# Layer 1: the first eight heads between the projection units of the last eight

## The chip, the core and the metric

The program runs on one core of one Trainium2 chip. A core has a tensor engine (PE), a vector engine (DVE), a scalar engine (ACT), a gpsimd engine (POOL) and a sync engine (SP) that issues transfers. Each engine works off its own queue in order and waits for the others through semaphores. The metric is the device time of one execution in microseconds (us). The kernel before takes 1052.06 us in the median of three runs (1048.58 to 1052.34).

## What is computed

Two blocks of two layers each, on 256 tokens of width 1024, in float32. The change is in layer 1 of the first block: normalise, project to q, k and v of 16 heads of width 64, turn q and k by position (rope), attend with a causal mask that holds the logarithm of how many of three patterns contain a key, project out, add. Cut to that:

```python
h = rms_norm(x, attn_norm[1])
q, k, v = split(h @ w_qkv_o)                  # 3 x 16 heads x 64
q, k = apply_rope(q, cos, sin), apply_rope(k, cos, sin)
for window, dil in ((128, 1), (512, 4), (2048, 16)):
    o, lse = banded_attention(strided(q), strided(k), strided(v), window // dil)
o = sum(softmax(lses) * outs)                 # merged by the softmax denominators
x = x + o @ w_out_o
x = x + silu_gated_ffn(rms_norm(x, ffn_norm[1]))
```

## The kernel before

**Split weights.** Float32 products are made of three products of rounded halves. Weights stream in units of 128 x 1024 elements through a ring of 8 slots: SP issues the transfer into `w_raw`, ACT makes the high half (`w_hi`, line 600), and DVE (line 885) or, for units listed in `POOL_UNITS`, POOL (line 492) makes the low half `w_lo` over the raw data. A slot is free again when PE has used the unit. ACT and DVE work four units ahead (`AHEAD`). `w_qkv_o` has 6 chunks of 512 columns and 4 units each, `w_out_o` has 2 chunks of 4 units. One unit is 12 matmuls on PE: 2 token tiles x 2 slices x 3 products (lines 1468 to 1470).

**Projection.** PE's `chunk` adds four units up in a pair of PSUM banks; ACT (line 654) and DVE (line 944) copy the sums to `z`, a token tile each. Chunks alternate between bank pair 0, 1 and bank pair 2, 3. Chunks 0 and 1 are q, 2 and 3 are k, 4 and 5 are v. After chunks 0 to 3 DVE's `rotate` applies rope (lines 977 to 984) and signals `qk1_ready`; after each of chunks 1 to 4 PE transposes two fills (`transpose_blocks`, line 1447). A fill is one PSUM bank of transposed blocks, numbered on through the whole program; even ones are drained by ACT (line 646), odd ones by DVE (line 934), and PE opens a fill only when the last one of its parity is drained (`open_fill`).

**Attention.** Only when all six chunks are done does `attention("attn1")` run over 16 heads, on each engine as one loop over steps. For every head: scores on PE (S, line 1609); mask, negative maximum and copy to SBUF on DVE (line 1017); two exponentials with row sums on ACT (lines 700 and 702); reciprocal and two scalings on DVE (lines 1058, 1065, 1066; the helper `scale_probs`); three transposes on PE (T, line 1654) into a fill; a copy to `probT` by ACT (line 715, even fills) or DVE (line 1041, odd fills); product with v on PE (PV, line 1634). For each pair of heads ACT (line 740) and DVE (line 1084) write the high and low half of the result to `hT_hi` and `hT_lo`. Then `project_out` multiplies with `w_out_o`, and the residual, norm and feed-forward follow. The 8 units of `w_out_o` are POOL's (line 492).

Of the kernel before, what the change touches and what calls it, by code (L numbers as in the profile page):

```python
# [5 lines left out]
F32 = mybir.dt.float32  # L6
# [28 lines left out]
def cut(lo, hi):  # L35
# [7 lines left out]
    "w_qkv_o": (cut(0, 3072), []),  # L43
# [62 lines left out]
FILL, _f = {}, 0  # L106
for _name, _n in [("norm0", 4), ("prep0", 11), ("cmp_p", 1), ("attn0", 24), ("norm1", 4), ("norm2", 4),
                  ("prep1", 8), ("attn1", 16), ("norm3", 4), ("norm5", 4), ("prep2", 7), ("attn2", 16),
                  ("norm6", 4), ("lora", 2), ("prep3", 12), ("attn3", 16)]:
    FILL[_name] = _f  # L110
    _f += _n
# [26 lines left out]
def net(nc, a, out):  # L138
# [30 lines left out]
    gains = place("gains", [P, GAIN_COLS])  # L169
    gtab = place("gtab", [P, NT, 4, HD])  # L170
    gb = place("gb", [P, D])
# [4 lines left out]
    w2 = place("w2", [P, 2, 192])  # L176
# [7 lines left out]
    reg = place("reg", [P, 24, T])  # L184
    prob_at = cursor[0]
    prob = place("prob", [P, 3, 512])
    probT = place("probT", [P, 2, 512])
# [224 lines left out]

    def bank_taken(p):
# [18 lines left out]
    POOL_UNITS = {st: (next_units(st), next_units(st) + RING) for st in STAGES}  # L432
# [40 lines left out]
    def _(pool):  # L473
# [37 lines left out]
        pool.wait_ge(t_filled, FILL["norm0"] + 4)  # L511
# [10 lines left out]
        split("attn1")  # L522
# [66 lines left out]
    def _(act):  # L589
# [28 lines left out]
        def high(k, t):  # L618

            for q in range(2):  # L620
                f = FILL[f"norm{k}"] + 2 * t + q
# [18 lines left out]
        def drain(stage, fills):  # L640
            for k in fills:
                f = FILL[stage] + k
# [6 lines left out]
        def take(name, c, dst, dense=None, done=None):  # L649
# [4 lines left out]
            n.activation(dst[0][:, 0, lo:lo + w], ps[:, 2 * (d % 2), 0:w], ACT.Copy).then_inc(acc_free[0], 1)  # L654
# [6 lines left out]
        def gate_chunks(name, which, dense):  # L661

            for g, c in enumerate(which):
# [3 lines left out]
                for b in range(4):  # L667
                    d = dense + 2 * g + b // 2
                    n.activation(gT[:, 4 * g + b, :], ps[:, 2 * (d % 2) + b % 2, 0:T], ACT.Silu)\
# [19 lines left out]
        def attention(stage):  # L689
            inst, i0, f0 = INST[stage], INST0[stage], FILL[stage]  # L690
            base = next_units(stage)
            for s in range(len(inst) + LAG + 5):
                if s < len(inst):
# [5 lines left out]
                    src, sign = (ps, 1.0) if it["bias"] is None else (prob, -1.0)  # L699
                    n.activation(prob[:, i % 3, 0:w], src[:, i % 3, 0:w], ACT.Exp, bias=negm[:, i, 0:1],  # L700
                                 scale=sign, accum_out=den[:, i, 0:1])
                    n.activation(prob[:, i % 3, 256:512], src[:, i % 3, 256:512], ACT.Exp, bias=negm[:, i, 1:2],
# [6 lines left out]
                if 0 <= j < len(inst) and (f0 + j) % 2 == 0:  # L709
# [5 lines left out]
                    n.activation(probT[:, i % 2, 0:w], ps[:, TB, 0:w], ACT.Copy).then_inc(t_drained[0], 1)  # L715
# [1198 lines left out]
```

## Times and profile before

| | before |
|---|---|
| median of three runs | 1052.06 us |
| the profiled execution, its own time | 1052.18 us |
| its span in the trace | 1050.4 us |
| TensorE clock granted, mean | 0.946 |
| DVE busy | 63% of the span |
| ACT busy | 46% of the span |

How to read the profile: busy time says how long an engine worked in a stretch; what a stretch is worth has to be read from the waits in it. Start times are counted from the span's start. The time of a matmul in the list is a latency; what it costs in a stream is the spacing of starts. A granted clock of 1.00 is 2.4 GHz, 0.50 is 1.2 GHz. The 1.8 us between span and device time lie around the program.

### The profile page before, as it was taken

The numbers are of one execution on the slowest core, as the hardware profiler recorded it, in microseconds if no ns is written. First come the engines' busy times: TensorE is split into PE (matmuls) and PEld (weight loads), VectorE is DVE, ScalarE is ACT, GpSimd is POOL, SyncE is SP. The second block draws the span as 40 slices with busy tenths as digits, with TensorE's granted clock in tenths as the row PEclk, the third lists the DMA queues.
The fourth block names the chain that finished last, engine by engine and source line by source line (L and its number), as shares of the span: only waits on it lengthen the run. The fifth ranks groups of instructions, "written<-read, shape, count | busy, mean of one in ns | idle before, by whom it ended". The sixth has DMA issues, their size and how long they took to land. (4 is left out here: it accounts for less than half of the span.)

```text
span 1050.4 us, 14873 instructions
## 1 busy us (share of the span) xinstructions
PE 934.8 (89%) x5660; PEld 795.0 (76%) x5660; DVE 664.3 (63%) x1200; ACT 484.5 (46%) x887; POOL 180.1 (17%) x129
## 2 busy tenths in 40 slices
PE   5995778899999999987899999998998799786878
PEld 4784446799998878855699999886887478586657
DVE  4778894456555458757545555546874947848672
ACT  5343653445454344455445545434544635442640
POOL 2004020000000000051000000003655300518430
PEclk9997779899999999989999999998999999998789
DMA  8463002465566657520546555656752036452001
GB/s 316 133 213 139 1 1 81 131 200 171 177 203 209 189 164 217 181 84 13 174 131 203 164 181 205 208 169 172 246 170 94 1 93 203 141 144 97 1 1 40
DMA packets 96790, 148.69 MB, mean 142 GB/s; under 512 B 6272, under 2 KB 59680, under 8 KB 96592
## 3 DMA queue, kind: packets, MB, share of 16 engines
q1 hardware_dynamic: 94512, 140.50, 42.6%
q10 hardware_dynamic: 1296, 4.83, 1.4%
q0 software_dynamic: 912, 2.41, 0.9%
q8 instruction: 45, 0.74, 0.3%
q14 instruction: 25, 0.20, 0.1%
HBM read 146.67 MB, written 1.05 MB: 141 GB/s over the span
## 5 line engine op out<-in xcount | busy, mean ns | idle before, releaser
L885 DVE TENSOR_TENSOR w_lo<-w_raw,w_hi 128x1024 fp32r<-128x1024 f32 (+2 forms) x230 | 272.3, 1208 | 150.3 <-ACT w_hi L600 147.3
L600 ACT ACTIVATE w_hi<-w_raw 128x1024 fp32r<-128x1024 f32 (+2 forms) x269 | 273.5, 1042 | 165.7 <-DMA w_raw<-in_w_gate_up 74.5
L1468 PE MATMUL ps<-hT_hi,w_lo 128*128 128x256 f32 x832 | 239.6, 288 | 8.5 <-POOL w_lo L492 4.6
L1469 PE MATMUL ps<-hT_hi,w_hi 128*128 128x256 f32 x832 | 239.1, 287 | 0.0
L1470 PE MATMUL ps<-hT_lo,w_hi 128*128 128x256 f32 x832 | 239.1, 287 | 0.0
L1468 PE MATMUL ps<-w_hi,hT_lo 128*128 128x512 f32 (+3 forms) x448 | 174.4, 389 | 9.2 <-DVE w_lo L885 4.4
L1469 PE MATMUL ps<-w_hi,hT_hi 128*128 128x512 f32 (+3 forms) x448 | 171.4, 383 | 0.0
L1470 PE MATMUL ps<-w_lo,hT_hi 128*128 128x512 f32 (+3 forms) x448 | 171.3, 382 | 0.0
L1468 PEld LDWEIGHTS ps<-hT_hi,w_lo 128*128 128x128 f32 x832 | 163.5, 196 | 9.6 <-issue 6.8
L1470 PEld LDWEIGHTS ps<-hT_lo,w_hi 128*128 128x128 f32 x832 | 163.4, 196 | 0.0
L1469 PEld LDWEIGHTS ps<-hT_hi,w_hi 128*128 128x128 f32 x832 | 163.2, 196 | 0.0
L492 POOL TENSOR_TENSOR w_lo<-w_raw,w_hi 128x1024 fp32r<-128x1024 f32 (+1 forms) x39 | 97.9, 2526 | 193.5 <-ACT w_hi L600 193.3
L1468 PEld LDWEIGHTS ps<-w_hi,hT_lo 128*128 128x128 f32 x448 | 85.9, 192 | 28.5 <-DVE w_lo L885 6.3
L1470 PEld LDWEIGHTS ps<-w_lo,hT_hi 128*128 128x128 f32 x448 | 85.7, 191 | 15.7
L1469 PEld LDWEIGHTS ps<-w_hi,hT_hi 128*128 128x128 f32 x448 | 85.8, 191 | 14.6
L1654 PE MATMUL ps<-table,prob 128*128 128x128 f32 x248 | 50.1, 326 | 35.1 <-DVE prob L1066 34.6
L1654 PEld LDWEIGHTS ps<-table,prob 128*128 128x128 f32 x248 | 30.5, 159 | 62.0 <-DVE prob L1066 52.7
L1468 PE MATMUL ps<-w_hi,hid_lo 128*128 128x512 f32 x176 | 69.6, 395 | 0.0
L1470 PE MATMUL ps<-w_lo,hid_hi 128*128 128x512 f32 x176 | 69.5, 395 | 0.0
L1469 PE MATMUL ps<-w_hi,hid_hi 128*128 128x512 f32 x176 | 69.5, 395 | 0.0
L498 POOL TENSOR_TENSOR small<-small 128x1 f32<-128x1 f32 x10 | 5.6, 556 | 326.6 <-DVE small L892 326.6
L654 ACT ACTIVATE z<-ps 128x512 f32<-128x512 f32 (+3 forms) x20 | 11.2, 562 | 93.1 <-PE ps L1470 93.1
(207 smaller groups left out, 1148.8 us busy)
## 6 DMA issues: line engine op xcount, KB each, us to landing
w_raw<-in_w_gate_up SPq DMA_DIRECT2D x176, 256.0 KB, 4.4
w_raw<-in_w_down SPq DMA_DIRECT2D x44, 512.0 KB, 4.2
w_raw<-in_w_in_e SPq DMA_DIRECT2D x38, 512.0 KB, 4.9
w_raw<-in_w_qkv_o SPq DMA_DIRECT2D x24, 512.0 KB, 4.0
w_raw<-in_w_in_o SPq DMA_DIRECT2D x20, 512.0 KB, 3.6
w_raw<-in_w_out_e SPq DMA_DIRECT2D x16, 512.0 KB, 5.1
w_raw<-in_w_out_o SPq DMA_DIRECT2D x16, 512.0 KB, 3.7
w_raw<-in_w_in_e SPq DMA_DIRECT2D x8, 268.0 KB, 2.7
```

Of the source, the lines that this page charges most:

```text
L492: g.tensor_tensor(w_lo[:, u % RING, 0:size], w_raw[:, u % RING, 0:size], w_hi[:, u % RING, 0:size].bitcast(F32), ALU.subtract).then_inc(po ...
L498: g.tensor_tensor(rstd[:, t:t + 1], ms[:, t:t + 1], halfs[:, 0:1], ALU.pow)\
L600: n.activation(w_hi[:, u % RING, 0:size], w_raw[:, u % RING, 0:size], ACT.Copy).then_inc(hi_ready, 1)
L654: n.activation(dst[0][:, 0, lo:lo + w], ps[:, 2 * (d % 2), 0:w], ACT.Copy).then_inc(acc_free[0], 1)
L885: v.tensor_tensor(w_lo[:, u % RING, 0:size], w_raw[:, u % RING, 0:size], w_hi[:, u % RING, 0:size].bitcast(F32), ALU.subtract).then_inc(lo ...
L1468: m.matmul(o, lhs[1], rhs[0], start=start, stop=False)
L1469: m.matmul(o, lhs[0], rhs[0], start=False, stop=False)
L1470: return m.matmul(o, lhs[0], rhs[1], start=False, stop=stop)
L1654: ins = m.transpose(ps[:, TB + f % 2, col:col + P], prob[:, i % 3, 256 * t + kt * P:256 * t + kt * P + P], ident)
```

## The change

The columns of `w_qkv_o` are taken in the order q, k, v of heads 0 to 7, then q, k, v of heads 8 to 15. After chunk 2, all four engines walk one table, `HEADS_1`, and each picks the events that are its own. `unit` is one projection unit (on ACT and DVE: the halves of the unit four further on), S n the scores, maxima and exponentials of heads 2n and 2n+1, SC n their scaling, T j the transposes and copy of head j, PV n and MIX n the product with v and the halves of the result, `take` the copy of a chunk's sums, `rope` the rotation, `fill` the transposes of q and k, `out` a unit of `w_out_o`.

```diff
-    "w_qkv_o": (cut(0, 3072), []),
+    "w_qkv_o": ([(1024 * p + 512 * half, 512) for half in range(2) for p in range(3)], []),
+SHARED = [DENSE["w_qkv_o"] + c for c in (3, 4, 5)]
+BANK = {d: 2 * (d % 2) for d in range(_d)}
+BANK.update({d: 0 for d in SHARED})
+for _name in OUTS:
+    BANK[DENSE[_name]], BANK[DENSE[_name] + 1] = 0, 2
+HEADS_1 = [("unit", 3, 0), ("unit", 3, 1), ("S", 0), ("unit", 3, 2), ("unit", 3, 3), ("SC", 0), ("take", 3), ("S", 1),
+           ("T", 0), ("T", 1),
+           ("unit", 4, 0), ("unit", 4, 1), ("SC", 1), ("rope", 3), ("S", 2), ("T", 2), ("T", 3), ("PV", 0),
+           ("unit", 4, 2), ("unit", 4, 3), ("SC", 2), ("take", 4), ("MIX", 0), ("S", 3), ("T", 4), ("T", 5), ("PV", 1),
+           ("unit", 5, 0), ("unit", 5, 1), ("SC", 3), ("rope", 4), ("fill", 2), ("fill", 3), ("MIX", 1), ("T", 6),
+           ("T", 7), ("PV", 2),
+           ("unit", 5, 2), ("MIX", 2), ("fill", 6), ("fill", 7), ("S", 4), ("unit", 5, 3), ("PV", 3), ("take", 5),
+           ("SC", 4), ("MIX", 3), ("S", 5), ("T", 8), ("T", 9),
+           ("out", 0), ("SC", 5), ("S", 6), ("T", 10), ("T", 11), ("PV", 4),
+           ("out", 1), ("SC", 6), ("MIX", 4), ("S", 7), ("T", 12), ("T", 13), ("PV", 5),
+           ("SC", 7), ("MIX", 5), ("T", 14), ("T", 15), ("PV", 6), ("MIX", 6), ("PV", 7), ("MIX", 7)]
-    POOL_UNITS = {st: (next_units(st), next_units(st) + RING) for st in STAGES}
+    POOL_UNITS = {st: (next_units(st), next_units(st) + RING) for st in STAGES if st != "attn1"}
-    prob = place("prob", [P, 3, 512])
-    probT = place("probT", [P, 2, 512])
+    prob = place("prob", [P, 4, 512])
+    probT = place("probT", [P, 4, 512])
```

The accumulators of chunks 3, 4 and 5 and of the first chunk of `w_out_o` share banks 0 and 1, since the scores now stand in banks 2 and 3, a head each: S n waits for the maxima of S n-1. `prob` and `probT` have four buffers. In layer 1 ACT alone makes the copies to `probT`, of both parities, and the result goes to buffers of its own (`mixed_hi`, `mixed_lo`), so that `hT` stays readable. The low halves of `w_out_o` move from POOL to DVE. On PE and DVE the walk is, in its main branches:

```diff
+                if what == "unit":
+                    split(FIRST["w_qkv_o", at[0]] + at[1] + 1 + AHEAD)
+                elif what == "out":
+                    split(FIRST["w_out_o", 0] + at[0] + 1 + AHEAD)
...
+                elif what == "rope":
+                    rope_1(at[0])
+                elif what == "fill":
+                    drain("prep1", at)
+                elif what == "S":
+                    maximum("attn1", 2 * at[0])
+                    maximum("attn1", 2 * at[0] + 1)
+                elif what == "SC":
+                    scale_probs("attn1", 2 * at[0])
+                    scale_probs("attn1", 2 * at[0] + 1)
...
+        def transposed(stage, j):
+
+            i, f, causal = INST0[stage] + j, FILL[stage, j], INST[stage][j]["causal"]
+            pe.wait_ge(probs_ready, i + 1)
+            open_fill(f)
```

**Where instructions stand.** First DVE, before, from the end of chunk 2 to the halves that follow: the sums, rope, the odd fill, four low halves.

```order
L944 COPY z<-ps 128x512 [waits units_used]
L977 TENSOR_TENSOR tmp<-z,table 128x16x32 [waits acc_free_1,acc_free_0]
L979 TENSOR_TENSOR tmp<-z,table 128x16x32
L982 TENSOR_TENSOR z<-z,table 128x2x512 [waits dve_chain]
L984 TENSOR_TENSOR z<-z,tmp 128x2x512 [waits dve_chain]
L934 COPY reg<-ps 128x512 [waits dve_chain,t_filled]
L885 TENSOR_TENSOR w_lo<-w_raw,w_hi 128x1024 [waits hi_ready] x4
```

DVE in the change, at the table's `unit 5,0` to `MIX 2`: two low halves, SC 3 (six rows, the last three shown), rope 4, the odd fill (fill 3), MIX 1.

```order
L967 TENSOR_TENSOR w_lo<-w_raw,w_hi 128x1024 [waits hi_ready] x2
...
L1184 RECIPROCAL fac<-den 128x2 [waits exp_ready]
L1191 TENSOR_SCALAR prob<-prob,fac 128x128 [waits dve_chain]
L1192 TENSOR_SCALAR prob<-prob,fac 128x256
L1059 TENSOR_TENSOR tmp<-z,table 128x16x32 [waits acc_free_1,acc_free_0]
L1061 TENSOR_TENSOR tmp<-z,table 128x16x32
L1064 TENSOR_TENSOR z<-z,table 128x2x512 [waits dve_chain]
L1066 TENSOR_TENSOR z<-z,tmp 128x2x512 [waits dve_chain]
L1016 COPY reg<-ps 128x512 [waits dve_chain,t_filled]
L1211 TENSOR_TENSOR mixed_lo<-ps,mixed_hi 128x256 [waits mix_hi]
```

The odd fill still follows a rope, and in front of both now stand the scalings of two heads.

PE in the change, at the table's `fill 2` to `unit 5,2`: fills 2 and 3 (line 1573), T 6 and T 7 (line 1784), PV 2 (line 1769), the next unit.

```order
L1573 MATMUL ps<-table,z 128x128 [waits t_drained_even,qk1_ready]
L1573 MATMUL ps<-table,z 128x128 x3
L1573 MATMUL ps<-table,z 128x128 [waits t_drained_odd,qk1_ready]
L1573 MATMUL ps<-table,z 128x128 x3
L1784 MATMUL ps<-table,prob 128x128 [waits t_drained_even,probs_ready]
L1784 MATMUL ps<-table,prob 128x128 x2
L1784 MATMUL ps<-table,prob 128x128 [waits t_drained_odd,probs_ready]
L1784 MATMUL ps<-table,prob 128x128 x2
L1769 MATMUL ps<-probT,z 64x256 [waits t_drained_odd,t_drained_even,mix_lo]
L1769 MATMUL ps<-probT,z 64x256
L1769 MATMUL ps<-probT,z 64x128 x2
L1594 MATMUL ps<-w_hi,hT_lo 128x512 [waits lo_ready]
```

Before, only projection units stood behind a pair of fills; now a head's transposes do, in the same two banks.

ACT in the change, from S 3 to the units' high halves behind it (`S 3`, `T 4`, `T 5`, `unit 5,0`, `unit 5,1`, the even fill).

```order
L825 ACTIVATE prob,den<-prob,negm 128x128 [waits max_ready]
L827 ACTIVATE prob,den<-prob,negm 128x256
L825 ACTIVATE prob,den<-prob,negm 128x128 [waits max_ready]
L827 ACTIVATE prob,den<-prob,negm 128x256
L837 ACTIVATE probT<-ps 128x384 [waits pv_done,t_filled] x2
L643 ACTIVATE w_hi<-w_raw 128x1024 [waits units_used,slot_full_6]
L643 ACTIVATE w_hi<-w_raw 128x1024 [waits units_used,slot_full_7]
L689 ACTIVATE reg<-ps 128x512 [waits t_filled]
```

Two heads' exponentials and two copies stand in front of the weights' high halves; before, the four high halves of a chunk stood in a row with nothing of the attention near them.

## Rows read from the trace of the kernel before

**Rows 1.** Busy time by stage; columns in the first line, then one stage a line.

```profile
core 0: us, PE busy (x) PEld busy (x) DVE busy (x) ACT busy (x) POOL busy (x), PEclk, DMA share, GB/s
420.80:455.50 34.70, 34.70 (x163) 28.59 (x160) 20.12 (x22) 14.02 (x17) 9.48 (x4) 1.00 0.59 180
455.50:493.30 37.80, 27.57 (x177) 16.43 (x176) 32.05 (x128) 26.33 (x85) 9.41 (x4) 0.82 0.05 16
493.30:504.20 10.90, 10.90 (x50) 9.03 (x49) 1.65 (x2) 2.36 (x3) 0.00 (x0) 1.00 0.41 126
```

**Rows 2.** Timeline of PE, two fills, then projection units: start, time, line, shapes.

```profile
420.00 1.03 PE L1447 MATMUL ps<-table,z 128*128 128x128 f32 x8
420.80 0.48 PE L1468 MATMUL ps<-w_hi,hT_lo 128*128 128x512 f32 x1
```

**Rows 3.** Timeline of PE in the attention's last part and the first out unit.

```profile
485.76 0.93 PE L1609 MATMUL ps<-reg 64*128 64x128 f32 x8
486.65 0.55 PE L1654 MATMUL ps<-table,prob 128*128 128x128 f32 x3
487.21 0.87 PE L1634 MATMUL ps<-probT,z 128*64 128x256 f32 x8
...
492.52 0.87 PE L1634 MATMUL ps<-probT,z 128*64 128x256 f32 x8 [0.74 <-DVE probT L1041]
493.32 0.50 PE L1468 MATMUL ps<-w_hi,hT_lo 128*128 128x512 f32 x1
```

**Rows 4.** Timeline of DVE: rope of one chunk, a fill, four low halves.

```profile
409.23 0.69 DVE L977 TENSOR_TENSOR tmp<-z,table 128x512 f32<-128x512 f32 x1
...
413.19 0.69 DVE L934 COPY reg<-ps 128x512 f32<-128x512 f32 x1
413.80 4.62 DVE L885 TENSOR_TENSOR w_lo<-w_raw,w_hi 128x1024 fp32r<-128x1024 f32 x4
```

**Rows 5.** Timeline of DVE: one head of attention, the next head's start, a low half.

```profile
459.77 0.28 DVE L1017 CUSTOM_DVE_ANT_0 prob<-ps,table 128x128 f32<-128x128 f32 x1
...
460.32 0.16 DVE L1058 RECIPROCAL fac<-den 128x2 f32<-128x2 f32 x1
...
460.99 0.28 DVE L1017 CUSTOM_DVE_ANT_0 prob<-ps,table 128x128 f32<-128x128 f32 x1
...
484.97 0.42 DVE L1084 TENSOR_TENSOR hT_lo<-ps,hT_hi 128x256 fp32r<-128x256 f32 x1
```

**Rows 6.** Timeline of ACT: four high halves, two heads' first exponentials, a copy.

```profile
432.96 3.91 ACT L600 ACTIVATE w_hi<-w_raw 128x1024 fp32r<-128x1024 f32 x4
...
458.09 0.40 ACT L700 ACTIVATE prob<-prob,negm 128x128 f32<-128x128 f32 x1 [0.64 <-DVE negm L1017]
...
458.98 0.39 ACT L700 ACTIVATE prob<-prob,negm 128x128 f32<-128x128 f32 x1
...
461.33 0.47 ACT L715 ACTIVATE probT<-ps 128x384 f32<-128x384 f32 x1
461.70 0.39 ACT L700 ACTIVATE prob<-prob,negm 128x128 f32<-128x128 f32 x1
```

**Rows 7.** Timeline of POOL and DVE where both work.

```profile
463.70 2.36 POOL L492 TENSOR_TENSOR w_lo<-w_raw,w_hi 128x1024 fp32r<-128x1024 f32 x1 [8.35 <-ACT w_hi L600]
...
464.40 1.74 DVE L1065 TENSOR_SCALAR prob<-prob,fac 128x128 f32<-128x128 f32 x1
```

**Rows 8.** Busy time and granted clock of single microseconds, columns as in Rows 1.

```profile
460.00:461.00 1.00, 0.46 (x3) 0.22 (x3) 0.96 (x8) 0.56 (x3) 0.00 (x0) 0.80 0.00 0
470.00:471.00 1.00, 1.00 (x8) 0.47 (x4) 1.00 (x1) 0.64 (x4) 1.00 (x1) 0.58 0.00 0
...
523.00:524.00 1.00, 1.00 (x5) 1.00 (x6) 0.48 (x1) 0.91 (x1) 0.00 (x0) 0.50 0.75 213
528.00:529.00 1.00, 1.00 (x7) 1.00 (x7) 0.81 (x1) 0.28 (x1) 0.00 (x0) 0.56 0.01 4
```

**Rows 9.** Waits of PE in the attention: for whom, total us, times, longest.

```profile
PE ps L1654 <- DVE prob L1066: 7.6, 9, 1.9
```

More of the change, by code:

```diff
@@ L786, in _ @@
         load_gain(3, 2)
-        for c in range(6):
-            chunk("w_qkv_o", c, z1)
-            if 1 <= c < 5:
-                drain("prep1", range(2 * c - 2, 2 * c))
-        attention("attn1")
+        chunk("w_qkv_o", 0, z1)
+        chunk("w_qkv_o", 1, z1)
+        drain("prep1", (0, 1))
+        chunk("w_qkv_o", 2, z1)
+        drain("prep1", (4, 5))
+        heads_1()
         projection_out("w_out_o")
@@ L929, in drain @@
             for k in fills:
[L930 removed]
+                f = FILL[stage, k]
                 if f % 2:
@@ L1049, in attention, with maximum, heads_1, rope_1 @@
                     at_step(s)
+        def maximum(stage, j):
+            i, it = INST0[stage] + j, INST[stage][j]
+            dve.wait_ge(scores_ready, i + 1)
+            if j >= 4:
+                dve.wait_ge(t_filled, FILL[stage, j - 4] + 1)
+            for t in range(NT):
+                w = P * (t + 1) if it["causal"] else T
+                cols = slice(256 * t, 256 * t + w)
+                ins = v.tensor_tensor_reduce(out=prob[:, i % 4, cols], in0=ps[:, 2 + i % 2, cols], in1=it["bias"](t),
+                                             scale=-1.0, scalar=-4.0 * NEG, op0=ALU.add, op1=ALU.min,
+                                             accum_out=negm[:, i, t:t + 1])
+            ins.then_inc(max_ready, 1)
+        def heads_1():
+            for what, *at in HEADS_1:
+                if what == "unit":
+                    split(FIRST["w_qkv_o", at[0]] + at[1] + 1 + AHEAD)
+                elif what == "out":
+                    split(FIRST["w_out_o", 0] + at[0] + 1 + AHEAD)
+                elif what == "take":
+                    take(DENSE["w_qkv_o"] + at[0], z1, *COLS["w_qkv_o"][0][at[0]], LAST["w_qkv_o", at[0]])
+                elif what == "rope":
+                    rope_1(at[0])
+                elif what == "fill":
+                    drain("prep1", at)
+                elif what == "S":
+                    maximum("attn1", 2 * at[0])
[3 more added lines that the diff above has]
+                    scale_probs("attn1", 2 * at[0] + 1)
+                elif what == "MIX":
+                    mix_low("attn1", 2 * at[0] + 1)
+        def rope_1(c):
+            wait_taken("w_qkv_o", c + 1)
+            lo = COLS["w_qkv_o"][0][c][0]
+            sec = heads(z1[:, :, lo:lo + 512])
+            rotate(sec, [sec], rope_q if lo < 1024 else rope, 8, 32)
+            dve.sem_inc(sem("qk1_ready"), 1)
         def scale_probs(stage, j):
@@ L1215, in _ @@
         norm_second(2, EPS_1)
-        for c in range(6):
-            chunk("w_qkv_o", c, z1)
-            if c < 4:
-                sec = heads(z1[:, :, 512 * c:512 * c + 512])
-                rotate(sec, [sec], rope_q if c < 2 else rope, 8, 32)
-                dve.sem_inc(sem("qk1_ready"), 1)
-            if 1 <= c < 5:
-                drain("prep1", range(2 * c - 2, 2 * c))
-        attention("attn1")
+        chunk("w_qkv_o", 0, z1)
+        rope_1(0)
+        chunk("w_qkv_o", 1, z1)
+        rope_1(1)
+        drain("prep1", (0, 1))
+        chunk("w_qkv_o", 2, z1)
+        drain("prep1", (4, 5))
+        heads_1()
         projection_out("w_out_o", 2, 3, EPS_1)
```

265 lines of the change are left out of this document (167 added, 98 removed).

## Prediction, written before the change was run

> **What bounds the kernel now.** I read the stages first [rows 1]. In the projection PE is busy all the time: 34.7 of 34.7 us in chunks 3 to 5, at full clock. In the attention it is busy 27.6 of 37.8 us, at a mean clock of 0.82, and the first chunk of `w_out_o` is dense again from 493.3 to 504.2. So the idle time is in the attention, and what ends most of it is the scaling of the probabilities on DVE: 7.6 us in 9 waits [rows 9]. DVE is busy 32.1 of 37.8 us there, but only 20.1 of 34.7 us beside chunks 3 to 5, and ACT 14.0 [rows 1]: there is room in the projection for attention work. Part of DVE's time is a block by POOL: a low half on POOL from 463.70 to 466.06 holds DVE's scaling, begun at 464.40, for 1.74 us [rows 7]; the same scaling takes 0.2 us from start to start elsewhere. There are four such halves in the stage.
>
> **Prices.** On PE, start to start at full clock: a unit 2.72 us (10.9 us for four [rows 1]), two fills 0.80 [rows 2], scores of two heads 0.89, transposes of a head 0.56, a pair's PV 0.80 [rows 3]. On DVE: maxima of a head 0.55, its scaling 0.67, a result's low half 0.35, a weight's low half 1.16, rope 3.96, a copy of 512 columns 0.61 [rows 4, 5]. On ACT: exponentials of a head 0.89, a copy to `probT` 0.37, a high half 0.98 [rows 6].
>
> **What would be won if PE never waited.** From the start of chunk 3, at 420.8 in both [rows 2] (the order of the first three chunks leaves two pairs of fills before it in both, and the rope that goes from behind chunk 2 only frees DVE), PE has up to the end of the first chunk of `w_out_o` 16 units 43.5, two pairs of fills 1.6, scores 7.1, transposes 8.5, PV 6.4: 67.1 us, end at 487.9 instead of 504.2. That is the whole prize, 16.3 us. After that point nothing changes: the next transfers into the ring, the residual add and the norm follow the units of that chunk as before, so an end moved by d moves the program by d.
>
> **What it costs: the order on DVE and ACT.** The table puts work of the weights and of the heads into one in-order queue on each of the two, and each waits for the other within one period. From the maxima of S n to those of S n+1: maxima of the first head 0.55, two heads' exponentials 1.78, two copies to `probT` 0.75 (these sit on ACT behind the exponentials), the first high half with its handover 1.1, two low halves 2.32, SC 1.34. That is 7.84 us in which nothing of PE appears. I add this chain up in the clock of the trace of before:
>
> - S 0's maxima: 420.8 + two units 5.44 + scores 0.85 = 427.1.
> - To S 1: 7.84, without the copies (-0.75), with the take of chunk 3 (+0.61): 434.8.
> - To S 2: 7.84 and rope 3, which stands ahead of S 2: 3.96. 446.6.
> - To S 3: 7.84, take 0.61, MIX 0.35: 455.4. PE ended unit 4,3 at about 449.7 and the scores of S 3 at 450.6, and T 4 waits for SC 2's first head at about 453.7: 3 us idle.
> - To fill 3 drained: 7.84, rope 4 3.96, the copy 0.69: 467.9. Here is the longest wait. T 7 writes the bank that fill 3 was in, and DVE drains fill 3 only behind rope 4. PE is through with unit 5,1 and both fills at about 462 and with T 6 at 463, so it is idle nearly 5 us.
> - To S 4's maxima: now PE is the path: T 7 0.56, PV 2 0.80, unit 5,2 2.72, fills 6 and 7 0.80, their drain 0.65, scores 0.85: 474.3.
> - To S 5: 0.55, 1.78, high half 1.1, one low half 1.16, take 0.61, SC 1.34, MIX 0.35: 6.9, at 481.2. To S 6: no take and no MIX, but two copies: 6.7, at 487.9. To S 7: 7.0, at 494.9. PE has a unit, scores, two T and a PV in such a period, 5.5 us: it waits, with 1 to 2.5 us of slack.
> - To the end: 0.55, 1.78, 0.67 to the scaling of head 15, 497.9; T 15 0.56 and two PV 1.60, 500.0; two units of `w_out_o` 5.45: 505.5.
>
> Against 504.2 that is 1.3 us later: the waits, some 17.6 us in sum, eat the whole prize. The table-load and the exponentials hidden beside chunk 3 are in the chain; the low halves of `w_out_o` that DVE takes from POOL are 1.16 each in it, and the blocks by POOL are gone from it. The step I trust least is the sum of handovers, taken from start-to-start times; 2 us either way.
>
> **The clock.** In the trace the clock falls to 0.50 at 460 to 461, in the attention's thin beginning, and is back at 1.00 only late in 470 to 471; and before the feed-forward, where PE had waited for the norm, a dense stream runs at 0.50 from 523 until 528.9 [rows 8]. Such a stretch at half clock costs a PE-bound stream half its length. The change removes the first stretch (it is inside the 37.8 us, so its price is already in the comparison), and makes a new gap of 5 us before T 7. I expect the fall there. T 7 to the fills are 4.9 us of work at full clock and all on the path. The bounds are nothing and 4.9 us; I take the dense case's length of 5.6 us, hence 2.8 us, since what follows T 7 is a stream like that one. The fall that I also expect behind the gap before T 4 is hidden: units 5,0 and 5,1 and the fills have until 467.9.
>
> Sum: 1.3 + 2.8 = 4.1 us. The profiled execution took 1052.2 (span 1050.4 and 1.8 around it), the median is 1052.06, the same to 0.1; forecast 1056.3.
>
> **The rest at no cost.** Banks 0 and 1 shared by chunks 3, 4, 5: PE's next unit waits for the take, but S n+1 and two T stand between, and the chain already holds the take. Scores in two banks: S n waits for maxima that are over by then. The other three attentions get more buffers with unchanged waits. The transfers: the ring's slots come free as before, and in the attention DMA was at 0.05 [rows 1].
>
> **Rivals.**
>
> - The clock also falls at the tail. Between PV 5 (495.9) and 500 PE has only T 14, T 15 and the first of PV 6 and 7, and the two units behind them are on the path. Another 2.8 us: 1059.1. For it: a thin stretch like 459 to 461. Against it: in before the end of the attention was as thin and 493.3 to 504.2 is at 1.00 [rows 1]. The Trainium skill, "TensorE: Matmul & The Clock Gate", Part 4 on PE-mode transposes, says that transposes do not count as activity for the clock as matmuls do. By that rule this tail, where half the work is transposes, falls and the time is the 1059.1 of this rival; no row here separates transposes from other work, so it only adds to the chance.
> - The clock stays up, or the gap before T 7 is shorter: 1.3 us alone, 1053.5, and with the chain 2 us too long 1051.
> - The change does what its words say and PE hardly waits: 1035.9. This needs DVE and ACT to run ahead of the chain. Against it: rope 4 stands in the queue before the drain, in any timing.
> - Slower by one mechanism: PE stays at half clock from T 7 on for as long as the longest stretch seen, 10 us [rows 8]. Then T 7 to the fills cost 4.9 more, and with S 4 and unit 5,3 at half clock (7.2 us) `take 5` is no longer hidden by the 5.4 us of the exponentials and halves beside it: 1.8 more. With 1.3 that is 8.0: 1060.2. It decides from the point where unit 5,3 at half clock ends later than DVE's low half.
>
> **How the numbers follow.** Forecast 1056.3 with 0.42 (its own spread 1053.8 to 1058.8), the tail's clock 0.20, the clock up 0.17, as meant 0.06, the long half clock 0.15. A change of over 0.5%, 5.3 us, is about what a measurement can tell from none; its bound above is 1057.3. Above it lie 0.12 of the forecast, 0.17 of the second and 0.14 of the last: slower 0.43. Faster (under 1046.8) is the case as meant and a little of the clock case, 0.10. The rest, 0.47, is within. The range from 1049.5 to 1062 leaves out the case as meant and the outer parts of two others.
>
> **What would show it.** Right: PE idle about 5 us before the transposes of head 7, ended by DVE's copy to `reg`; about 3 us before T 4, ended by DVE's scaling; PE waiting 1 to 2 us in each of the last four periods of about 7 us; PE busy well under all of 421 to 500; low clock behind T 7; DVE's scaling nowhere over 0.4 us. Wrong: a wait before T 7 under 2 us, or a first chunk of `w_out_o` that ends before 500. If it ends near 505 but the time differs, the error is behind that point, where I expect no change.

## The result, and the profile after

| | before | after |
|---|---|---|
| median | 1051.69 us (20 runs) | 1058.72 us (20 runs) |
| lowest, highest | 1047.77, 1058.06 us | 1047.37, 1066.66 us |
| the profiled execution | 1052.18 us, span 1050.4 | 1057.84 us, span 1056.0 |
| mean granted clock in it | 0.946 | 0.945 |

The ratio after to before is 1.0055, with a 95% interval of 1.0034 to 1.0076: 3.6 to 8.0 us slower, 5.8 in the middle. The medians of the table are 7.0 us apart; they hold all 20 executions of after, while the ratio leaves out the two slowest (1066.08 and 1066.66 us). The forecast was 1056.3 us, 4.1 slower than before; the measured median lies 2.4 us above it, within the forecast's range of 1049.5 to 1062.

To compare layer 1 alone, this text uses its **length**: from the second pair of fills, at 420.00 in before [rows 2] and 425.57 in after, to the first transposes of the norm behind `w_out_o`, at 515.04 and 524.78. It is 95.0 us before and 99.2 after, 4.2 longer. Times of after are moved back by 5.57 us where they are set against those of before.

First the stages, at the clock times of [rows 1] (columns as there). They cut the same intervals from the span, though the program is 5.6 us behind:

```profile
core 0: us, PE busy (x) PEld busy (x) DVE busy (x) ACT busy (x) POOL busy (x), PEclk, DMA share, GB/s
420.80:455.50 34.70, 33.44 (x170) 25.63 (x168) 21.93 (x52) 15.36 (x38) 0.00 (x0) 1.00 0.47 148
455.50:493.30 37.80, 28.43 (x151) 20.14 (x150) 21.88 (x60) 18.02 (x47) 0.00 (x0) 0.91 0.22 74
493.30:504.20 10.90, 7.60 (x50) 4.90 (x48) 7.28 (x30) 4.51 (x15) 0.00 (x0) 1.00 0.32 96
```

PE's idle time was in the middle stage alone, 10.2 us; now it is in all three, 13.9 us. DVE, busy 32.05 of 37.80 us before, is busy 21.88: it is not the bound by its busy time any more, nor is ACT. POOL has left the stage. Now the waits of PE in layer 1 of after (for whom, total us, times, longest), which answer to [rows 9]:

```profile
PE ps L1784 <- DVE prob L1192: 8.9, 5, 3.4
PE ps L1784 <- DVE reg L1016: 3.1, 1, 3.1
PE ps L1784 <- ACT probT L837: 1.9, 1, 1.9
PE ps L1743 <- ACT reg L689: 0.8, 1, 0.8
```

The nine waits of at most 1.9 us for the scaling (7.6 us in all) have become five, of up to 3.4 (8.9 in all), and one of 3.1 for the odd fill's bank has come. The timeline of PE shows where they are (start, latency, line, shapes, idle before and who ended it): the transposes of T 4, T 6 and T 7, and then one wait in each of the last four periods. A **period** here is the time from the maxima of S n on DVE to those of S n+1. The first of the five waits, 0.93 us at T 2, is not shown.

```profile
459.94 1.21 PE L1784 MATMUL ps<-table,prob 128*128 128x128 f32 x6 [3.40 <-DVE prob L1192]
...
470.40 0.52 PE L1784 MATMUL ps<-table,prob 128*128 128x128 f32 x3 [0.34 <-ACT reg L689]
474.04 0.52 PE L1784 MATMUL ps<-table,prob 128*128 128x128 f32 x3 [3.12 <-DVE reg L1016]
...
488.59 1.20 PE L1784 MATMUL ps<-table,prob 128*128 128x128 f32 x6 [1.46 <-DVE prob L1192]
...
495.64 1.21 PE L1784 MATMUL ps<-table,prob 128*128 128x128 f32 x6 [2.20 <-DVE prob L1192]
...
502.37 1.21 PE L1784 MATMUL ps<-table,prob 128*128 128x128 f32 x6 [0.87 <-DVE prob L1192]
506.27 0.89 PE L1784 MATMUL ps<-table,prob 128*128 128x128 f32 x6 [1.89 <-ACT probT L837]
```

Why DVE's scaling is late can be read on ACT's and DVE's own timelines of after. One turn: the maxima of S 2 on DVE, exponentials, copies and high halves on ACT, low halves and the scaling SC 2 on DVE.

```profile
452.60 0.29 DVE L1142 CUSTOM_DVE_ANT_0 prob<-ps,table 128x128 f32<-128x128 f32 x1 [0.25 <-DVE z L1066]
...
453.28 0.40 ACT L825 ACTIVATE prob<-prob,negm 128x128 f32<-128x128 f32 x1 [7.41 <-DVE negm L1142]
...
455.05 0.84 ACT L837 ACTIVATE probT<-ps 128x384 f32<-128x384 f32 x2
455.79 1.99 ACT L643 ACTIVATE w_hi<-w_raw 128x1024 fp32r<-128x1024 f32 x2
...
456.87 2.36 DVE L967 TENSOR_TENSOR w_lo<-w_raw,w_hi 128x1024 fp32r<-128x1024 f32 x2 [3.07 <-ACT w_hi L643]
459.15 0.16 DVE L1184 RECIPROCAL fac<-den 128x2 f32<-128x2 f32 x1
...
461.39 0.28 DVE L1142 CUSTOM_DVE_ANT_0 prob<-ps,table 128x128 f32<-128x128 f32 x1
```

DVE is idle for 3.07 us before the low halves, because the first high half stands on ACT behind exponentials and copies that begin only with DVE's maxima; ACT was idle for 7.41 us before the exponentials. Each of the two waits for the other in every period, and the scaling, whose inputs were there from 455.2 on, stands behind the low halves till 459.15. The sum over the sixteen heads of after (426.3 to 515 us), two rows of the waits of all engines:

```profile
ACT prob L825 <- DVE negm L1142: 28.6, 8, 7.4
DVE w_lo L967 <- ACT w_hi L643: 22.8, 10, 3.1
```

### The profile page after: what moved, and what is told of

Read it like the earlier page. It is cut to its first block and busy times, and to the rows that moved or that the text cites. A ratio compares the mean times of both kernels' runs of the same rounds, so it can differ in the third digit from the quotient of the medians.

```text
span 1056.0 us, 14877 instructions
## 1 busy us (share of the span) xinstructions
PE 935.9 (89%) x5660; PEld 794.0 (75%) x5660; DVE 662.5 (63%) x1200; ACT 487.1 (46%) x895; POOL 160.5 (15%) x121
## 5 line engine op out<-in xcount | busy, mean ns | idle before, releaser
L967 DVE TENSOR_TENSOR w_lo<-w_raw,w_hi 128x1024 fp32r<-128x1024 f32 (+2 forms) x238 | 282.1, 1209 | 167.8 <-ACT w_hi L643 164.4
L1594 PE MATMUL ps<-w_hi,hT_lo 128*128 128x512 f32 (+3 forms) x416 | 163.1, 392 | 8.5 <-DVE w_lo L967 4.4
L1595 PE MATMUL ps<-w_hi,hT_hi 128*128 128x512 f32 (+3 forms) x416 | 159.3, 383 | 0.0
L1596 PE MATMUL ps<-w_lo,hT_hi 128*128 128x512 f32 (+3 forms) x416 | 159.0, 382 | 0.0
L1594 PEld LDWEIGHTS ps<-w_hi,hT_lo 128*128 128x128 f32 x416 | 80.2, 193 | 28.5 <-issue 6.8
L536 POOL TENSOR_TENSOR w_lo<-w_raw,w_hi 128x1024 fp32r<-128x1024 f32 (+1 forms) x31 | 78.7, 2554 | 120.9 <-ACT w_hi L643 120.6
L1596 PEld LDWEIGHTS ps<-w_lo,hT_hi 128*128 128x128 f32 x416 | 79.9, 192 | 14.8
L1595 PEld LDWEIGHTS ps<-w_hi,hT_hi 128*128 128x128 f32 x416 | 80.3, 193 | 13.4
L1784 PE MATMUL ps<-table,prob 128*128 128x128 f32 x248 | 47.0, 311 | 42.9 <-DVE prob L1192 36.6
L1743 PE MATMUL ps<-reg 64*128 64x256 f32 (+2 forms) x288 | 44.6, 408 | 5.4 <-ACT reg L689 2.6
```

The costliest lines, as they stand in the source:

```text
L536: g.tensor_tensor(w_lo[:, u % RING, 0:size], w_raw[:, u % RING, 0:size], w_hi[:, u % RING, 0:size].bitcast(F32), ALU.subtract).then_inc(po ...
L967: v.tensor_tensor(w_lo[:, u % RING, 0:size], w_raw[:, u % RING, 0:size], w_hi[:, u % RING, 0:size].bitcast(F32), ALU.subtract).then_inc(lo ...
L1594: m.matmul(o, lhs[1], rhs[0], start=start, stop=False)
L1595: m.matmul(o, lhs[0], rhs[0], start=False, stop=False)
L1596: return m.matmul(o, lhs[0], rhs[1], start=False, stop=stop)
L1743: ins = m.matmul(o, it["q"][:, t * P:(t + 1) * P], it["k"][:, 0:w], start=True, stop=True)
```

## The experiments

All are the changed kernel with one or two edits, except "only outside layer 1", in which layer 1 is as before. The lengths of layer 1 are from one profile each. Each ratio is to executions of the kernel before taken beside that kernel; for the experiments these were three sets, with medians of 1051.49 to 1053.30 us.

| kernel | layer 1, us | median, us | ratio | 95% interval |
|---|---|---|---|---|
| before | 95.0 | 1051.69 | | |
| after | 99.2 | 1058.72 | 1.0055 | 1.0034 to 1.0076 |
| fill before rope | 94.4 | 1051.88 | 1.0012 | 0.9981 to 1.0043 |
| only outside layer 1 | 95.7 | 1051.56 | 0.9996 | 0.9965 to 1.0027 |
| ACT two units ahead | 82.3 | 1037.92 | 0.9878 | 0.9834 to 0.9922 |
| the same, again | 82.4 | 1038.23 | 0.9880 | 0.9829 to 0.9930 |
| ACT one unit ahead | 88.8 | 1046.04 | 0.9940 | 0.9911 to 0.9969 |
| two ahead, fill before rope | 81.8 | 1040.84 | 0.9898 | 0.9855 to 0.9940 |
| one ahead, fill before rope | 84.0 | 1043.86 | 0.9916 | 0.9881 to 0.9952 |
| low halves on POOL | 93.2 | 1049.36 | 0.9976 | 0.9946 to 1.0006 |
| low halves on POOL, two ahead | 90.0 | 1045.48 | 0.9935 | 0.9899 to 0.9971 |
| high halves twice | 112.9 | 1065.66 | 1.0125 | 1.0091 to 1.0158 |
| high halves twice, two ahead | 86.7 | 1044.62 | 0.9939 | 0.9906 to 0.9972 |

### Is anything lost outside layer 1?

The profile of after is 6.05 us longer inside attention 0 (the attention of the first layer, from its first fills to the norm behind it), where the waits are nearly the same. So the parts outside layer 1 were kept, and layer 1 was put back:

```diff
-    "w_qkv_o": ([(1024 * p + 512 * half, 512) for half in range(2) for p in range(3)], []),
+    "w_qkv_o": (cut(0, 3072), []),
...
-SHARED = [DENSE["w_qkv_o"] + c for c in (3, 4, 5)]
...
-BANK.update({d: 0 for d in SHARED})
...
-    POOL_UNITS = {st: (next_units(st), next_units(st) + RING) for st in STAGES if st != "attn1"}
+    POOL_UNITS = {st: (next_units(st), next_units(st) + RING) for st in STAGES}
...
+        split("attn1")
...
```

> The changed kernel with layer 1 put back as before (column order, banks, hand-over of heads, GpSimd's share of the low halves), and with all that it changed elsewhere kept: four buffers of prob and probT, the banks of the out units, the second weight tile. Theory (all of the loss is in layer 1; the 6 us that the profile shows inside attention 0 are a clock that differs from execution to execution): ratio to the kernel before 0.999 to 1.001. Rival (the parts outside layer 1 cost something): 2 to 6 us over the kernel before, with the first attention longer in the profile.

Measured: 0.9996, layer 1 95.7 us. The parts outside cost nothing that can be measured (the interval reaches 3.5 us less to 2.8 us more); what is lost is lost in layer 1. The 6 us inside attention 0 are taken up in the last section.

### Does T 7 wait for DVE's order?

```diff
-           ("unit", 5, 0), ("unit", 5, 1), ("SC", 3), ("rope", 4), ("fill", 2), ("fill", 3), ("MIX", 1), ("T", 6),
+           ("unit", 5, 0), ("unit", 5, 1), ("SC", 3), ("fill", 2), ("fill", 3), ("rope", 4), ("MIX", 1), ("T", 6),
```

> One change in the table: VectorE drains the transposes of fills 2 and 3 before rope 4 instead of behind it, so that the bank that T7 needs comes free 3.96 us sooner. Theory (VectorE's order makes T7 late, and TensorE's clock falls behind that wait): T7 waits under 1 us, the granted clock stays at 1.00 behind it, and the eight exps of heads 8 to 15 come about 5.8 us earlier; less what the later waits for VectorE's scaling take back, the time is about 3 to 5 us below the changed kernel's (1058.7), so 1053.5 to 1055.5. Rival (T7's wait is slack, the chain of scalings is late on its own): no change against 1058.7. Rival (the rope is now what the scores of group 4 wait for): the wait moves from T7 to S4, time within 1 us of 1058.7.

Measured: layer 1 94.4 us, 4.9 shorter than after; ratio 1.0012, so some 4.5 us less than after, though the two intervals overlap (1.0034 to 1.0043). The wait of T 7 is gone, the clock stays at 1.00 where it fell behind T 7 in after, and what is left of after's waits is that of the chain, nearly unchanged:

```profile
PE ps L1784 <- DVE prob L1192: 8.8, 5, 3.4
PE ps L1784 <- ACT probT L837: 1.9, 1, 1.9
PE ps L1743 <- ACT reg L689: 1.1, 1, 1.1
```

The scores of S 4 start 51.2 us behind the second fills instead of 56.0. The theory holds by the profile: T 7's wait lay on the path. Neither rival does: the wait was no slack, and S 4's scores wait only 0.3 us longer for ACT's copy than in after.

### Is the period a chain between the two engines?

This is the main question, since by it the prediction let the whole prize go. ACT's high halves are moved in its own queue and nowhere else; DVE and PE walk the table as in after. The edit moves those of the whole table, not only those of heads 8 to 15 of which the expectation speaks.

```diff
                 if what == "unit":
-                    split(FIRST["w_qkv_o", at[0]] + at[1] + 1 + AHEAD)
+                    split(FIRST["w_qkv_o", at[0]] + at[1] + 3 + AHEAD)
                 elif what == "out":
-                    split(FIRST["w_out_o", 0] + at[0] + 1 + AHEAD)
+                    split(FIRST["w_out_o", 0] + at[0] + 3 + AHEAD)
```

> ScalarE makes the high halves of heads 8 to 15 two units further ahead in its own order, so that VectorE's low halves no longer stand behind a high half of the same period. Theory (the last periods of about 7 us are a chain that passes from VectorE to ScalarE and back: 7.84 us with the high half in it, 4.8 us without): the four periods behind S3 shrink from about 6.9 us to what TensorE needs, about 6 us or less; the end of layer 1 comes 3 to 6 us earlier, time 1052.5 to 1055.5. Rival (VectorE's busy time alone is the bound, whatever ScalarE's order): no change, 1058.7. Rival (the splits ahead now delay exp and the copies of transposed probabilities on ScalarE by 1.1 us each): later by 1 to 3 us.

Measured: 1037.92 us, ratio 0.9878, and on another chip 0.9880 with 1038.23 us.

> The kernel with ScalarE two units further ahead once more, on this chip, beside the two others: ratio 0.985 to 0.990 to the kernel before, the layer 82 to 83 us from the second fills to the norm. If its first ratio of 0.9878 was a matter of the chip or of few executions, it will lie above 0.992.

Layer 1 takes 82.3 us (82.4 again), 16.9 less than after and 12.7 less than before. The direction was right, the size three to five times too small in my expectation (3 to 6 us): I had looked only at the periods behind S 3, and all seven from S 0 to S 7 shrink. The same turn as above, maxima of S 2 to the scaling, now on DVE:

```profile
441.92 0.29 DVE L1142 CUSTOM_DVE_ANT_0 prob<-ps,table 128x128 f32<-128x128 f32 x1 [0.25 <-DVE z L1066]
...
443.04 2.35 DVE L967 TENSOR_TENSOR w_lo<-w_raw,w_hi 128x1024 fp32r<-128x1024 f32 x2
```

The low halves follow the maxima at once (443.04; in after 3.07 us of idle time lay between), because their high halves were made a period earlier, and the exponentials run beside them on ACT. DVE's waits for high halves fall from 22.8 us to this:

```profile
DVE w_lo L967 <- ACT w_hi L643: 4.0, 3, 2.3
```

And PE waits 3.5 us in the sixteen heads instead of 15.0 (the rows of after above, and those of 0.93 us at T 2 and 0.83 at S 4). One row without a wait, T 12 and T 13 at 479.87, is shown as well:

```profile
456.91 0.52 PE L1784 MATMUL ps<-table,prob 128*128 128x128 f32 x3 [0.34 <-ACT reg L689]
458.32 0.52 PE L1784 MATMUL ps<-table,prob 128*128 128x128 f32 x3 [0.89 <-DVE reg L1016]
...
464.29 0.93 PE L1743 MATMUL ps<-reg 64*128 64x128 f32 x8 [0.83 <-ACT reg L689]
...
479.87 0.88 PE L1784 MATMUL ps<-table,prob 128*128 128x128 f32 x6
...
483.03 0.89 PE L1784 MATMUL ps<-table,prob 128*128 128x128 f32 x6 [1.48 <-ACT probT L837]
```

The granted clock is 1.00 throughout:

```profile
420.00:455.00 35.00, 35.00 (x187) 26.86 (x186) 28.77 (x78) 24.36 (x56) 0.00 (x0) 1.00 0.45 141
455.00:501.00 46.00, 42.45 (x245) 31.71 (x244) 31.03 (x83) 25.11 (x66) 0.55 (x1) 1.00 0.30 98
```

Of the 16.9 us, 11.5 are waits of PE that are gone. Another 3.4 are stretches at half clock that are gone: in after, read in pieces of 2 us, the mean clock is 0.86, 0.50 and 0.79 behind T 4 and 0.77, 0.50 and 0.87 behind T 7, so each stretch lacks 1.7 us of work at full clock. Of the last 2.0 us some 1.8 are in the transposes. In after the scaling of T 13 ends at 502.97, behind the start of T 12 at 502.37, and the pair takes 1.13 us to the next work; with ACT ahead it takes 0.81 (479.87 to 480.68). The pairs at T 0, T 2, T 4, T 8 and T 10 lose 0.15 to 0.34 us in the same way. The prediction's case "PE hardly waits" had layer 1 at 95.0 - 16.3 = 78.7 us; with the 3.5 us of waits above it is 82.2, and 82.3 was measured. So the sum of PE's work was right, and all of the prize but these waits can be had with the table as it is. Its terms were not all right: transposes were priced at 0.56 us a head (and entered as 8.5 us, where 16 times 0.56 is 9.0), and a pair takes 0.81 here; a unit behind other work takes 2.86 (459.57 to 462.43) instead of 2.72.

### One unit, or two?

```diff
-                    split(FIRST["w_qkv_o", at[0]] + at[1] + 1 + AHEAD)
+                    split(FIRST["w_qkv_o", at[0]] + at[1] + 2 + AHEAD)
```

(the same for `out`).

> ScalarE only one unit further ahead. The chain theory by its own terms: of a period's two high halves one still stands behind the exps, so from maxima to maxima it takes 0.55 + 1.78 + 1.1 + 1.16 + 1.34 = about 5.9 us, under the 7 to 8 us that TensorE works in the periods with two units and about its 5.4 in the last ones: 0 to 2 us above the run with two units ahead, 1038 to 1040. Rival (the gain grows with each unit ahead, because what counts is the sum of high halves ahead of an exp): half of the 20.8 us, about 1048.

Measured: layer 1 88.8 us, ratio 0.9940; against the run with two ahead 6.5 us more in the profile and about the same by the ratios. I had expected 0 to 2, and the time, 1046.04 us, lies nearer to the rival's 1048 than to my 1038 to 1040. The waits tell why:

```profile
PE ps L1784 <- DVE reg L1016: 3.6, 1, 3.6
PE ps L1784 <- DVE prob L1192: 1.8, 1, 1.8
PE ps L1784 <- ACT probT L837: 1.5, 1, 1.5
```

In the last four periods there is no wait for the scaling, as the chain of 5.9 us had it. But the four periods before are longer than PE's work by a little each, with rope 3 and 4 in them, and this adds up to 1.8 us at T 4 and to a late rope 4, behind which the bank of T 7 is drained: 3.6 us and a stretch at half clock behind it. The term that I had left out of the expectation is rope 4. The next kernel puts that to the test, one unit ahead and the fills drained first:

> ScalarE one unit further ahead, and fills 2 and 3 drained ahead of rope 4. With one ahead alone layer 1 from the second fills to the norm took 88.8 us against 82.3 with two ahead; its trace shows 3.6 us for T7 and 1.8 us ahead of T4, and no other wait that the run with two ahead has not. Theory (the rest of the difference is T7's bank and the clock behind that wait, the period itself is under TensorE's): T7's wait goes, the layer takes 84 to 85 us, time 2 to 3 us above the run with two ahead, ratio 0.990. Rival (the period is still bound by the one high half that stands behind the exps): waits move to T8 to T15, layer 87 to 89 us, ratio 0.994 as before.

Measured: 84.0 us and 0.9916. T 7 does not wait, and of the waits listed above only the 1.8 and the 1.5 us stay; the rival's waits at T 8 to T 15 don't appear. It is the profile that decides here: the interval of the ratio, 0.9881 to 0.9952, holds both the 0.990 of the theory and the 0.994 of the rival. Both together, two units ahead and the fills first:

> ScalarE two units further ahead, and VectorE drains fills 2 and 3 ahead of rope 4. In the run with ScalarE ahead alone T7 still waited 0.9 us for the bank and nothing else in the heads waited for VectorE, so the theory gives 0.5 to 1 us less than its 1037.9: 1037 to 1037.5, not to be told from it. Rival (with the chain gone, rope 4 later makes the scores of group 4 late, since the register copies and the rope now stand closer to them): up to 3 us more, 1041.

Measured: layer 1 81.8 us, 0.5 shorter than with two ahead alone, as expected; the median, 1040.84 us, is 3 us above the 1037 to 1037.5 expected, and the ratio 0.9898 (0.9855 to 0.9940) can't be told from 0.9878. With the chain gone, rope 4's place is worth half a microsecond; with the chain, 4.9. The three kernels with the fills first also answer the rival of the kernel with one unit ahead, that each unit gains alike: from 94.4 us the first unit ahead takes 10.4, the second only 2.2.

### Does a high half cost where it stands?

While the heads are worked off, ACT makes each high half twice, 14 of them in the table as changed, and 16 with ACT two units ahead:

```diff
...
+                if in_heads_1[0]:
+                    n.activation(w_hi[:, u % RING, 0:size], w_raw[:, u % RING, 0:size], ACT.Copy)\
+                     .then_inc(sem("twice"), 1)
+                    doubled[0] += 1
+                    act.wait_ge(sem("twice"), doubled[0])
                 n.activation(w_hi[:, u % RING, 0:size], w_raw[:, u % RING, 0:size], ACT.Copy).then_inc(hi_ready, 1)
...
```

> The changed kernel with each high half of ScalarE made twice while the heads are worked off (the second write repeats the first), some 1.1 us more for each of 14. Chain theory: both high halves of a period lie on the chain VectorE, ScalarE, VectorE, so nearly all of them show: 10 to 15 us more than the changed kernel's 1058.7, 1069 to 1073. Rival (ScalarE is only half busy, 46.6 of 92 us, and its time is covered): 0 to 3 us more.

> The same doubling in the kernel with ScalarE two units further ahead. Chain theory: the high halves lie beside VectorE's low halves and the scaling now, and ScalarE's own work in a period (exps 1.78, copies 0.75, two doubled high halves 4.2, about 0.6 of other copies: 7.3 us) stays under TensorE's 7 to 8: 0 to 4 us above 1037.9, 1038 to 1042. Rival (each high half costs wherever it stands): 10 to 15 us more, 1048 to 1053.

Measured on the changed kernel: layer 1 112.9 us in the profile, 13.7 more than after, within the 10 to 15 expected; but the median, 1065.66 us, is below the 1069 to 1073 expected. The two largest of PE's waits there:

```profile
PE ps L1792 <- DVE prob L1200: 15.3, 7, 5.4
PE ps L1792 <- DVE reg L1024: 4.8, 1, 4.8
```

They have grown by 8.1 us, and with them the stretches at half clock. By the ratios, 1.0125 against 1.0055, the doubling costs only 7.4 us, with some 3 to 11.5 left open by the two intervals taken together; the profiled execution, 1077.05 us, is the longest of the six. So that it costs is shown; that it costs more than the rival's 0 to 3 us is shown by the profile and only just by the ratios. The size in a typical execution is open.

With ACT two units ahead the same doubling costs 4.4 us in the profile (86.7 against 82.3), just above the 0 to 4 expected (median 1044.62 us, expected 1038 to 1042). It has two places: a copy of the sums, which now stands behind two doubled high halves, and the last copy to `probT`.

```profile
PE ps L1792 <- ACT probT L843: 3.0, 1, 3.0
PE ps L1602 <- ACT z L703: 2.6, 1, 2.6
```

None of it is a wait for the scaling. In the profiles the pair says what the chain theory does (13.7 against 4.4 us for the same work or more). The ratios, 7.4 and 6.4 us with intervals of four to six us around each, don't tell the two apart, and by them alone this pair would be inconclusive.

### Would POOL have been the better place for the low halves?

```diff
-    POOL_UNITS = {st: (next_units(st), next_units(st) + RING) for st in STAGES if st != "attn1"}
+    POOL_UNITS = {st: (next_units(st), next_units(st) + RING) for st in STAGES}
...
+        split("attn1")
...
```

> The low halves of the out projection's splits in layer 1 go back to GpSimd, where the kernel before had them; nothing else. Theory (VectorE's in-order chain carries 1.16 us for each of these, two in a period): the last periods lose up to 2.3 us each if VectorE alone is late, so the time is 2 to 5 us below the changed kernel's. Rival (the GpSimd instruction of 1.74 us holds VectorE's scaling back while it runs, or its half is late for TensorE): the wait goes from VectorE's scaling to GpSimd's half, time the same within 1 us or up to 3 us above 1058.7.

> ScalarE two units further ahead, and the low halves of the out projection back on GpSimd. Theory (with the high halves ahead TensorE waits for neither engine, so it does not matter who makes the low halves): layer within 1 us of 82.3, ratio 0.987 to 0.989. Rival (GpSimd's 1.74 us instructions hold VectorE's maxima and scaling back, or GpSimd's 2.0 us a half come late for units that now follow each other sooner): TensorE waits for a low half or for scaling, layer 84 to 87 us, ratio 0.990 to 0.993.

Measured: in the changed kernel the move back helps, layer 1 93.2 us and 0.9976, 6.1 us less than after in the profile and some 8 by the ratios (expected 2 to 5). With ACT ahead the same move hurts: 90.0 us against 82.3; the ratios, 0.9935 against 0.9878 and 0.9880, point the same way with overlapping intervals. The second is the rival's case, by more than the rival said, and it is to be seen on two lines of DVE, one of POOL and one of PE in that kernel:

```profile
452.36 3.30 DVE L1065 TENSOR_TENSOR z<-z,table 128x1024 f32<-128x1024 f32 x1
455.69 3.25 DVE L1067 TENSOR_TENSOR z<-z,tmp 128x1024 f32<-128x1024 f32 x1
...
452.12 5.73 POOL L536 TENSOR_TENSOR w_lo<-w_raw,w_hi 128x1024 fp32r<-128x1024 f32 x2 [2.94 <-ACT w_hi L644]
...
459.92 0.88 PE L1785 MATMUL ps<-table,prob 128*128 128x128 f32 x3 [4.15 <-DVE reg L1017]
```

The two large steps of rope 4 take 3.30 and 3.25 us beside two low halves on POOL; with POOL idle they take 1.22 us each, in the run with ACT ahead at the same place:

```profile
454.85 1.22 DVE L1064 TENSOR_TENSOR z<-z,table 128x1024 f32<-128x1024 f32 x1
456.11 1.22 DVE L1066 TENSOR_TENSOR z<-z,tmp 128x1024 f32<-128x1024 f32 x1
```

POOL's two halves take 5.73 us together, where one takes 2.36 [rows 7]. The times fit each waiting for the other's instruction in turn: POOL's first half would end at 454.48, DVE's step of 1.22 us behind it at 455.70, POOL's second half at 458.06 and DVE's second step at 459.28; DVE's ended at 455.66 and 458.94, POOL's second half at 457.85. (The 1.74 us that the expectations give to GpSimd's instruction is DVE's held scaling in [rows 7], and no run has the 2.0 us a half; POOL's own take 2.35 to 2.39 where nothing holds them.) The Trainium skill, "SBUF — State Buffer", section "Who interferes with whom", says that VectorE and GpSimd share a pair of ports under an exclusive lock, and that a VectorE instruction with two SBUF inputs contends with a GpSimd instruction that reads SBUF; these rows agree, with 2.0 and 2.1 us more for two instructions of 1.22. The 4 us land just where T 7's bank is drained, and T 7 waits 4.15 us, 3.3 more than with POOL idle. Most of the rest of the 7.7 us is a wait of 1.71 us for the scaling at T 8, which that run does not have, and the half clock behind T 7: from T 7 to the scores of S 4 it is 8.20 us instead of 5.97.

In the changed kernel with ACT where it was, rope 4 is stretched in the same way (3.30 and 3.28 us), but low halves are taken out of DVE's chain, in the periods that wait for it: PE's waits for the scaling fall from 8.9 us in five to 6.0 in three, and T 7's from 3.1 to 1.7. So by the profiles the change was right to take the low halves from POOL, once the chain is undone, and wrong on that before.

## Why the prediction was right, step by step

Times of after are moved back by 5.57 us.

- **The in-order chain, 7.84 us a period plus rope and takes.** Forecast and measured starts or ends: maxima of S 0 427.1 and 427.4, S 1 434.8 and 435.1, S 2 446.6 and 447.0, S 3 455.4 and 455.8, fill 3 drained 467.9 and 468.3. Each step to within 0.4 us, and 0.3 of it is there from S 0 on. The idle time before T 4 was put at 3 us, ended by DVE's scaling: 3.40, so ended.
- **The longest wait, T 7.** Its cause was right (DVE's copy to `reg`, behind rope 4), and what it costs stood the test of its own experiment. Its length was not: 3.12 us instead of 5. PE came to T 6 later than 463, at 464.8, since it had done units 5,0 and 5,1 at half clock behind T 4. The text had this fall and called it hidden, which it was: T 7's time is set by DVE. It should then have shortened its own wait.
- **S 4, and the clock.** 474.3 with 2.8 for the clock, 477.1; measured 477.0. Here two terms were off in opposite directions, and that they met so closely is luck. From fill 3 drained to the maxima of S 4 the forecast had 6.4 us at full clock and 2.8 for half clock. With ACT two ahead, at full clock all the way, T 7 to the scores of S 4 takes 5.97 us, in after 7.57: the half clock cost 1.6 us, not 2.8. In two other kernels the same way took 7.52 (one unit ahead) and 8.20 us (two ahead, low halves on POOL), so it cost 1.6 and 2.2: the term was too large in each. The step that I took from the dense stretch of before [rows 8], 5.6 us long, was a guess by likeness; the stretch here is shorter (clock 0.50 in the first, 0.73 in the second of these two pieces of after):

```profile
475.00:477.00 2.00, 2.00 (x11) 1.30 (x8) 0.94 (x1) 1.36 (x3) 0.00 (x0) 0.50 0.01 4
477.00:479.00 2.00, 2.00 (x8) 1.60 (x7) 0.62 (x2) 0.00 (x0) 0.00 (x0) 0.73 0.00 0
```

  The work at full clock was counted too small, by some 0.6 us: the scores of S 4 wait 0.83 us for ACT's copy to `reg`, and the copy was in the sum at 0.65 without its handover.
- **The last four periods.** S 5 481.2 + 2.8 = 484.0 and 483.9, S 6 490.7 and 490.6, S 7 497.7 and 497.65. First of the last two units 502.8 and 503.1. The waits of 1 to 2.5 us were 1.46, 2.20, 0.87 and 1.89.
- **Nothing behind this point, nothing outside.** Layer 1 is 4.17 us longer in the profiles against 4.1 forecast, closer than terms that were off by about 1 us earn, and the kernel with only the parts outside layer 1 is at 0.9996.
- **The clock in before.** The prediction has one stretch at half clock in the attention of before, at 460 to 471. There is a second, behind waits of PE of 1.27 and 1.90 us, that it did not count:

```profile
480.00:482.00 2.00, 0.77 (x3) 0.50 (x3) 2.00 (x8) 0.26 (x1) 0.83 (x1) 0.77 0.01 4
482.00:484.00 2.00, 2.00 (x11) 1.29 (x11) 1.40 (x9) 1.25 (x5) 0.00 (x0) 0.50 0.00 0
```

  Like the first it lies within the length of before that the forecast compares with, so the sum is not touched.
- **The rivals.** The tail's clock didn't fall: it is 1.00 from 479.57 (unmoved) to the end of layer 1 in after. The page that the prediction quotes for this rival, the Trainium skill's "TensorE: Matmul & The Clock Gate", Part 4, made it likelier; after shows no fall in that tail, in which 2.0 of PE's 4.5 us of work are transposes (501.5 to 509, unmoved). The case "as meant", 0.06, is the one worth coming back to. It was dismissed with the sentence that rope 4 stands ahead of the drain in any timing. That is so, and what was concluded from it is wrong: with ACT ahead rope 4 stands there still and T 7 waits 0.9 us. Its place in the queue costs what the queue is late by, and the lateness came from the chain. I had the chain, with the high half as a term of 1.1 us in it, and took the chain for a property of interleaving, when it is a property of one offset in ACT's walk. The forecast was right about this kernel and would have been wrong about the idea.

The verdict on the time itself is less sharp than that on the layer. The interval of 3.6 to 8.0 us holds both the 4.1 forecast and a change beyond 0.5%; the middle, 0.55%, lies just over that line; 0.47 of the chance had been put within it and 0.43 beyond.

## What to carry over

When two in-order engines hand work to each other in both directions within one period, write down the chain from one hand-over to the same one a period later: the time that counts is this sum, not the busy time of either (here 7.84 us, with DVE busy 61% and ACT 45% of the three stages). Then ask of each term whether its input is ready a period earlier; such work (here the high halves) goes ahead of the term that has to wait for the other engine, and one constant was worth 16.9 us of layer 1. And take a step on one queue that everything waits behind (rope 4) as a symptom first: ask why the queue is late there, before moving the step.

## What was not expected of the hardware

**The clock of attention 0 differs from execution to execution.** Up to the second fills of layer 1 the changed kernel and its variants run the same instructions, yet these fills start at 417.3 to 426.3 us in eleven profiles of them. Most of it arises in attention 0. First after, then the kernel with ACT two units ahead, the first 24 us of that attention:

```profile
94.00:118.00 24.00, 19.72 (x103) 14.91 (x105) 15.35 (x76) 8.07 (x25) 0.00 (x0) 0.50 0.00 1
```

```profile
94.00:118.00 24.00, 19.00 (x121) 13.61 (x121) 17.46 (x84) 9.43 (x30) 0.00 (x0) 0.63 0.00 1
```

In the one the clock is at its half level all the time, in the other it rises within it (before has 0.62 there). The norm behind attention 0 comes at 191.08 and 185.41. It is not the kernel: over the eleven profiles this mean runs from 0.50 (in four) to 0.67 for the same instructions, and the kernel with ACT two units ahead shows 0.63 in one profile and 0.53 in the other. What sets it is open. In the 20 executions of after the time roughly follows the mean clock: 1047.37 us at 0.953, 1049.89 at 0.950, 1058.34 at 0.939, 1066.66 at 0.933. Whoever compares two single profiles of such a kernel should compare lengths of stages, not their starts.

**Behind which gaps the clock fell.** In the eight pairs of heads of the variants it fell to 0.50 behind every wait of PE of 3.12 us or more (3.12 and 3.40 in after; 3.38, 3.40, 3.55 and 4.15 in others; 3.29, 4.76 and 5.37 with the high halves doubled). It stayed at 1.00 behind most shorter ones, of which the longest are 2.20 us in after, 2.51 with the high halves doubled, and 2.64 and 2.96 with that and ACT two ahead. But it also fell behind one of 2.10 us with the high halves doubled, and twice in the attention of before, where no wait is over 1.90 us and PE is idle again and again; so the length of the last wait does not decide it alone. Nor does a wait of one length have one price. Behind the same 3.40 us at T 4 the kernel with low halves on POOL has a stretch at half clock about twice as long as that of after, here two pieces from its middle:

```profile
455.78:457.78 2.00, 2.00 (x10) 1.19 (x11) 1.47 (x11) 1.50 (x7) 0.00 (x0) 0.50 0.00 0
457.78:459.78 2.00, 2.00 (x6) 1.59 (x5) 1.84 (x6) 2.00 (x6) 0.00 (x0) 0.50 0.00 0
```

The stretch behind T 7 in after, which lay on the path, cost 1.6 us more than the wait itself.
